# A two-layer decoder on one core: the first layer's values projected for all heads at once, ahead of the head pairs

## The reference, cut to what matters

```python
h = rmsnorm(x, mixer_norm[0])
parts = split_cols(h @ even_w_in[0], [ATTN_W] * N_DIL + [ATTN_W, ATTN_W, CROSS_WIDTH])   # 3 q, k, v, cross q
mix = mixer_dilated(parts[:N_DIL], parts[N_DIL], parts[N_DIL + 1], rel_bias)
cross = cross_attention(parts[N_DIL + 2], mem_n, w_mem_kv[0])
x = x + jnp.concatenate([mix, cross], axis=-1) @ w_out[0]
```

## Time and profile before

| | |
|---|---|
| median of 3 runs | 1532.45 us (1531.69 to 1534.11) |
| profiled execution: its own time | 1534.58 us |
| its span, first to last instruction | 1532.8 us |
| PE busy | 1513.6 us, 99% |
| VectorE, ScalarE, POOL busy | 86%, 73%, 6% |
| TensorE clock, mean granted | 0.996 |
| first projection of pair 0 starts | 37.96 us |
| layer 0's attention ends on PE | 231.1 us |

### The profile page before, as it was taken

The page is one execution under the profiler, slowest core; times in us unless marked ns, Lnnn a source line. Parts: engine busy times, 40 slices in busy tenths (PEclk is TensorE's granted clock), DMA queues, the critical chain, the costliest instruction groups (busy, mean ns, idle before and its releaser), DMA issues.

```text
span 1532.8 us, 25011 instructions
## 1 busy us (share of the span) xinstructions
PE 1513.6 (99%) x8132; PEld 1280.9 (84%) x8132; DVE 1316.3 (86%) x1783; ACT 1124.7 (73%) x1487; POOL 95.3 (6%) x70
## 2 busy tenths in 40 slices
PE   9999999999999999999999999999999999999997
PEld 8999978888898788888888888888888888888886
DVE  5788868777778879998998998998998998998997
ACT  6565566544557668788788888788788888878875
POOL 2422100000030000000000000000000000000000
PEclk9999999999999989999999999999999999999999
DMA  9944546666633579999999999999999999999992
GB/s 283 241 138 137 152 129 190 190 186 192 170 90 90 164 291 369 391 380 390 381 369 389 378 374 385 380 377 376 382 396 360 384 395 358 387 391 352 401 385 112
DMA packets 225973, 455.39 MB, mean 297 GB/s; under 512 B 12848, under 2 KB 119488, under 8 KB 225920
## 3 DMA queue, kind: packets, MB, share of 16 engines
q1 hardware_dynamic: 221712, 439.52, 79.5%
q0 software_dynamic: 4208, 15.22, 3.9%
HBM read 445.52 MB, written 9.18 MB: 297 GB/s over the span
## 4 chain that ended last, share of the span: by engine, by line
PE 93%; DVE 4%; ACT 1%; issue 1%; DMA 0%; SPq 0%; ACTq 0%; DVEq 0%
PE ps L815 26%; PE ps L817 26%; PE ps L816 26%; PE ps L1139 5%; PE ps L1141 3%; PE ps L1327 2%; PE ps L931 2%; PE ps L967 1%; PE ps L947 1%; DVE w_lo L1824 1%; PE ps L1269 0%; DMA big<-in_w_mem_kv 0%; DVE X L2030 0%; DVE small L1920 0%; DVE pr L2190 0%
## 5 line engine op out<-in xcount | busy, mean ns | idle before, releaser
L1824 DVE TENSOR_TENSOR w_lo<-big,w_hi 128x1024 fp32r<-128x1024 f32 (+1 forms) x830 | 977.6, 1217 | 121.4 <-ACT w_hi L1711 52.2
L1711 ACT CAST w_hi<-big 128x1024 fp32r<-128x1024 f32 x672 | 693.5, 1056 | 139.1 <-PE ps L817 135.5
L815 PE MATMUL ps<-w_hi,m_hi 128*128 128x512 f32 (+1 forms) x1008 | 392.6, 389 | 1.5 <-DVE w_lo L1824 1.3
L817 PE MATMUL ps<-w_hi,m_lo 128*128 128x512 f32 (+1 forms) x1008 | 389.7, 387 | 0.0
L816 PE MATMUL ps<-w_lo,m_hi 128*128 128x512 f32 (+1 forms) x1008 | 389.6, 386 | 0.0
L815 PEld LDWEIGHTS ps<-w_hi,m_hi 128*128 128x128 f32 x1008 | 189.5, 188 | 41.5 <-issue 4.3
L817 PEld LDWEIGHTS ps<-w_hi,m_lo 128*128 128x128 f32 x1008 | 189.5, 188 | 38.2
L816 PEld LDWEIGHTS ps<-w_lo,m_hi 128*128 128x128 f32 x1008 | 189.6, 188 | 36.9
L1364 ACT CAST w_hi<-big 128x1024 fp32r<-128x1024 f32 (+2 forms) x166 | 164.8, 1003 | 39.5 <-PE ps L817 32.4
L815 PE MATMUL ps<-w_hi,h_two 128*128 128x512 f32 (+1 forms) x464 | 182.1, 392 | 0.0
L817 PE MATMUL ps<-w_hi,h_two 128*128 128x512 f32 (+1 forms) x464 | 179.5, 387 | 0.0
(11 more groups left out here) (309 smaller groups left out, 1560.6 us busy)
## 6 DMA issues: line engine op xcount, KB each, us to landing
big<-in_odd_w_gate SPq DMA_DIRECT2D x112, 1024.0 KB, 7.3
big<-in_odd_w_up SPq DMA_DIRECT2D x112, 1024.0 KB, 7.7
big<-in_odd_w_down SPq DMA_DIRECT2D x112, 1024.0 KB, 7.6
big<-in_even_w_in SPq DMA_DIRECT2D x42, 512.0 KB, 4.3
big<-in_even_w_gate SPq DMA_DIRECT2D x22, 512.0 KB, 4.6
big<-in_even_w_up SPq DMA_DIRECT2D x22, 512.0 KB, 3.9
big<-in_even_w_down SPq DMA_DIRECT2D x22, 512.0 KB, 4.7
big<-in_w_out SPq DMA_DIRECT2D x20, 512.0 KB, 3.7
```

Source lines behind the costliest of these rows:

```text
L815: mm(dst, a[0], b[0], start=start, stop=False, **kw)
L817: return mm(dst, a[1], b[0], start=False, stop=stop, **kw)
L1711: nc.scalar.copy(w_hi[:, slot, :], ring[s][:, (u % 2) * UNIT:(u % 2 + 1) * UNIT]).then_inc(s_hi, 1)
L1824: return V.tensor_tensor(dst, src, lead.bitcast(F32), ALU.subtract)
```

## The change

- The values of all 16 heads are made before pair 0: eight units `("values", c)`, one per chunk of 128 input features, with full rows of 1024 value columns. The tokens' chunk is the loaded operand and the weights are streamed, so the values come out with tokens on partitions and are copied (four copies of 512 columns) into `XH`, from which `mix` reads them. `turn_values`, `vN` and two copies per pair go.
- A pair has four matrices instead of five. The step on PE is `p(0, 1, 2)`, `turn_probs(now, 0)`, `p(3)`, `turn_probs(now, 1)`, `scores(nxt)`, `mix(now)`. `third_read` is waited for at `p(1)` instead of `p(0)`.
- The second head's division moves from DVE to ACT (`second_probs`).
- For pair 1 the fourth low part comes after the first reading of scores; inside the steps there is no fifth low part after the reading.
- In pair 7's step PE makes output units 0 and 1 instead of unit 0; pair 8's step makes 2 and 3 instead of 1, 2 and 3.
- On ACT the second head's exponentials stand ahead of the second projection's copy.
- PE's steps are written out instead of looped.

```diff
+        for c in range(DC):
+            add(("values", c), (c + 2) % SLOTS)
         for g in range(PAIRS):
-            for m in range(NBR + 2):
+            for m in range(NBR + 1):
                 add(("pair", 0, g, m), m)
...
+            def values_unit(c):
+
+                w = split(0, 0, [U.at[("values", c)]], 1)
+                pe.wait_ge(s_nlo, DC * NORM_MIX0 + c + 1)
                 for t in range(TT):
-                    last = tr(value_bank(pair)[:, tok(t)], vT[:, tok(t)], ident)
-                last.then_inc(S["turned_v"], 1)
+                    if c == 0:
+                        pe.wait_ge(s_me, 2 * t + 2)
+                    for hf in range(2):
+                        last = mm3(value_bank(t, hf), part(HS, A_, c, tok(t)), part(w, A_, 0, slice(hf * 512, (hf + 1) * 512)),
+                                   c == 0, c == DC - 1, skip_group_check=True)
+                        if c == DC - 1 and (t, hf) != (1, 1):
+                            last.then_inc(s_vmade, 1)
+                last.then_inc(s_used, 1)
...
-                if isinstance(now.g, int) and now.g >= LATE:
-                    ahead = {LATE: ((), (0,)), LATE + 1: ((1, 2), (3,)), LATE + 2: ((4, 5), (6,))}[now.g]
+                if now.g >= LATE:
+                    ahead = {LATE: ((0,), (1,)), LATE + 1: ((2,), (3,)), LATE + 2: ((4, 5), (6,))}[now.g]
                     if not now.cross:
                         project(nxt, 0)
-                        turn_values(now)
                         project(aft, 0)
...
-                p(0)
-                turn_values(now)
-                p(1)
+                p(0, 1, 2)
                 turn_probs(now, 0)
-                p(2, 3)
+                p(3)
                 turn_probs(now, 1)
                 scores(nxt)
-                p(4)
                 mix(now)
...
+            def second_probs(pair):
+
+                S = s_at[0]
+                act.wait_ge(S["summed"], 2 * pair.g + 2)
+                act.wait_ge(S["dve_rden"], 2 * pair.g + 2)
+                for t, (a, b) in enumerate(((0, P), (P, CAUSAL))):
+                    last = A(probs(pair, 1)[:, a:b], tmp[:, a:b], ACT.Copy, scale=rden[:, 1, t:t + 1])
+                last.then_inc(S["probs"], 1)
...
                     e(0)
-                    values()
                     h(0)
+                    exps(now, 1)
                     e(1)
-                    exps(now, 1)
                     h(1)
+                    e(2)
                     probsT(now, 0)
-                    e(2)
+                    second_probs(now)
                     h(2)
                     e(3)
+                    h(3)
                     probsT(now, 1)
-                    h(3)
-                    e(4)
                     h(4)
```

More of the change, by code:

```diff
@@ L620, in stream_loads @@
                 span = range(1, PAIRS // 2)
+                for c in range(DC):
+                    load(0, 0, [U.at[("values", c)]], w_in[0][:, c:c + 1, (NBR + 1) * D:(NBR + 2) * D])
                 load_pair(pair_at(0, 0))
@@ L759, in _ @@
             mask_pair(0, 0, True)
-            u = U.at[("pair", 0, 1, NBR + 1)]
+            u = U.at[("pair", 0, 1, NBR)]
             mask_pair(1, 1, True)
@@ L957, in mix @@
                 elif pair.l == 0:
-                    pe.wait_ge(S["values"], pair.g + 1)
-                    v = vN[:, :, :]
+                    v = XH[:, :, pair.g * P:(pair.g + 1) * P]
                 else:
@@ L1035, in stream @@
                 first = pair_at(0, 0)
+                for c in range(DC):
+                    values_unit(c)
                 for m in range(first.mats):
-                    project(first, m, norm if m == 0 else None)
-                pe.wait_ge(s_me, 2 * 2)
+                    if m < 2:
+                        pe.wait_ge(s_vout, m + 1)
+                    project(first, m)
+                pe.wait_ge(s_vout, 2 * TT)
                 scores(first)
-                steps(pe, step)
+                for g in range(NPAIR):
+                    step(pair_at(0, g), *(pair_at(0, h) if h < NPAIR else None for h in (g + 1, g + 2)))
                 for ch in range(LATE, NPAIR):
@@ L1473, in e @@
                         evac((nxt, aft)[m], 0)
-                def values():
-                    if not now.cross:
-                        act.wait_ge(S["turned_v"], now.g + 1)
-                        nc.scalar.copy(vN[:, :, :].rearrange("p t n -> p (t n)"), value_bank(now)).then_inc(S["values"], 1)
                 exps(now, 0)
@@ L1544, in step_odd, with values_out, stream @@
                     mix_hi(g)
-            def stream(done):
+            def values_out(t, hf):
+                if (t, hf) != (1, 1):
+                    act.wait_ge(s_vmade, 2 * t + hf + 1)
+                else:
+                    act.wait_ge(s_used, U.at[("values", DC - 1)] + 1)
+                nc.scalar.copy(XH[:, t, hf * 512:(hf + 1) * 512], value_bank(t, hf)).then_inc(s_vout, 1)
+            def stream():
                 act.sem_inc(s_at[0]["probsT"], 1)
                 a, b = pair_at(0, 0), pair_at(0, 1)
-                for m in range(done, a.mats):
+                for c in range(2, DC):
+                    hi(0, 0, [U.at[("values", c)]])
+                for m in range(3):
                     hi_mat(a, m)
+                for t in range(TT):
+                    for hf in range(2):
+                        values_out(t, hf)
+                hi_mat(a, 3)
                 for m in range(a.mats):
@@ L1580, in _ @@
                 hi(0, 0, [U.at[("mem", n)]])
-            for m in range(3):
-                hi_mat(pair_at(0, 0), m)
+            for c in range(2):
+                hi(0, 0, [U.at[("values", c)]])
             mem_out(1)
             act.wait_ge(s_scrw, 16)
-            stream(3)
+            stream()
             def half_copy(i, first, ns):
@@ L1941, in head_probs @@
                     dve.wait_ge(S["probs_turned"], n + 1)
+                if pair.kind == "even" and hh:
+                    return
                 for t, (a, b) in enumerate(((0, n0), (n0, n0 + SEQ))):
@@ L1955, in step @@
                     low(0)
-                    if isinstance(now.g, int) and now.g == LATE:
-                        head_probs(now, 1)
-                        low(1)
-                    else:
-                        low(1)
-                        head_probs(now, 1)
+                    head_probs(now, 1)
+                    low(1)
                     low(2)
```

45 lines of the change are left out of this document (21 added, 24 removed).

## The result

The changed kernel takes 1537.88 us (median of 8 runs, 1536.59 to 1538.85); the kernel before takes 1534.06 us beside it (8 runs, 1531.37 to 1534.25). The ratio is 1.0029, 95% interval 1.0019 to 1.0038: slower by 0.29%, some 4.4 us (the medians differ by 3.8). I had forecast no change, and the median lies 0.3 us above the range. Of the 5.0 us between my 1532.9 and 1537.88, 1.6 come from the kernel before, whose median I had from three runs (1532.45); the other 3.4 are the change. The profiled execution took 1536.94 us, 2.36 more than that of before.

A forecast was written before the change was run, and what follows sets the result against it. PE, busy 99% of the span, was taken as the bound. Terms 22.1 - 2.4 - 0.7 - 19.4 + 0.8 summed to +0.4 us, giving 1532.9 us for the median, range 1530.3 to 1537.6.

The forecast's parts named there:

- Term 1: Values for all heads ahead of pair 0: 96 matmuls of 0.2306 us on PE add 22.1 us.
- Term 2: Pair 0: one matrix less, partly offset by an uncovered wait for the key's copy, saves 2.4 us.
- term 3: From pair 0's scores to pair 1's: less PE work, limited by DVE's fourth low part, saves 0.7 us.
- Term 4: Six steps from pair 1's scores to pair 7's: each 3.2 us shorter, at 15.61 us, saving 19.4 us.
- the walk from E: One step timed from a score block's end, E: ACT and DVE keep up, with no slack at the key's copy.
- Term 5: From pair 7's scores on: matmuls saved, but PE stands 3.7 us before output unit 0; adds 0.8 us.
- The rival of ScalarE: In the steps, ACT's division and cast delay the key's copy, 0.6 us a step: 1537.1 us, chance 0.13.
- The rival of the clock: After the 3.7 us stall in pair 7's step, PE's clock halves for 8.2 us: +4.1, 1537.0 us, chance 0.10.

The follow-up runs named there:

- bias_at_scores: Changed kernel, but POOL's three bias additions of a step wait for the next pair's scores instead of the second head's probabilities: 1534.50 us.
- copy_first_all: Changed kernel, but in every even step ScalarE copies the second projection ahead of the second head's exponentials: 1531.57 us.
- div_on_dve: Changed kernel, but with the second head's division back on VectorE: 1538.69 us.
- low3_behind: Changed kernel, but the fourth low part stands behind the reading of the next pair's scores in every step: 1540.94 us.
- before_collide: Kernel before the change, but POOL's bias additions wait for the second head's exponentials instead of its probabilities: 1549.82 us.
- copy_first_last: Changed kernel, but in pair 7's step alone ScalarE copies pair 9's query ahead of the second head's exponentials: 1533.96 us.
- key_covered: Changed kernel with POOL's additions at the scores, second projection's copy first, four matrices before both probability transposes, key copied before turned probabilities: 1533.85 us.

## Why the prediction was right and wrong

- **Term 1** (+22.1, measured +21.75): right. The 96 matmuls take 21.86 us (37.85 to 59.71), 0.228 each, close to the row's 0.2306; no load held them up. The rule with which the prediction gets 0.216 is given in the Trainium skill, "TensorE: Matmul & The Clock Gate", section "Back-to-back issue gap", for an isolated matmul and not for a stream of them; the trace gives 0.228.
- **Term 2** (-2.4, measured -2.31) and **term 3** (-0.7, measured -0.94): right. Pair 0's scores start at 71.89 where I had 72.1.
- **Term 4** (-19.4, measured -16.05): wrong, and with it the sign of the result. The step that failed is the walk from E, "DVE starts to read at E+0.35 and ends the second head's maxima at E+6.1", and its end, "So all fits". It priced every low part at its length alone, 1.25 us, and left POOL out. It also left out that the fourth matrix needs bank 4 back from the second query, whose copy the change had put behind the second head's exponentials; by the walk's own times (copy done some 0.35 after E+9.3, matrix at E+9.8) that would have cost nothing, and it is where the delay shows. In the trace the reading starts at E+1.08 and the exponentials end at E+9.9 (164.76), not E+9.3. Without the collision the step is 15.54, where I had 15.61: the blocks were right. The division, taken as 0.7, took 0.81 (166.59 to 167.40). Rows for the collision stood in the trace of before, the two quoted above: POOL's additions wait for exactly the probabilities that the change moves to another engine, and a low part beside them takes 1.61 us.
- **Term 5** (+0.8, measured +2.05): the gap was right (3.54 for 3.7), and the term lacked the slower matmuls behind it, 1.6 us.
- **The rival of ScalarE** (steps of 16.0 or more would "prove" it): the steps did come to 16.17, with another cause. `bias_at_scores` shows that ScalarE's work alone did not set them; `copy_first_all` shows that it is a part of the loop that did (0.28 us a step for one copy). I had tied a mechanism to a number that a second mechanism gives as well; only its releaser, the key's copy, would have told it apart, and the trace has another.
- **The rival of the clock** (+4.1, 0.10): it happened, at 1.6 us. That gap was forecast in the sum itself, so what follows it belonged there too, with more than a chance of 0.10. Its price was too high, because it took over the length of another stretch (8.2 us).
- **The range:** the terms named for it add up to 1530.5 and 1537.0, where the prediction writes 1530.3 and 1537.6.
- **The sum:** +0.4 forecast, +3.35 for the steps, +1.25 for the end and -0.5 for the smaller misses give the +4.5 of the table. Removing both causes gives 1529.80, 8.1 us under the changed kernel and 0.33% under the kernel before. The change holds a gain of some 4 us and gives away twice that in two orders that it did not need.

## What to carry to other kernels

When a change moves an operation to another engine, list every wait on its semaphore, also on engines that are idle 94% of the time, and ask what will run beside the work that it starts. A wait's place on the bound engine shows where the delay arrives, not where it is made: look for the loop among the other engines, and cut it there. And a gap of 2 us or more on PE is to be priced with the slower matmuls that may stand behind it: 1.6 us here, behind two of the five gaps of 2.16 us and behind each of the four of 3.5 us or more (there 1.6 to 2.4).

## What the runs showed of the hardware

- A VectorE operation with two SBUF inputs and a POOL addition of SBUF operands exclude each other, instruction by instruction: low parts of 1.22 us take up to 2.30, additions of 0.54 take 1.57, and POOL's of 1.28 take 2.27. VectorE's operations with a PSUM input (0.41, 0.55 and 0.68 us) and its maxima of one input (0.55 and 0.94) kept their lengths beside POOL in `bias_at_scores`.
- Who starts first decides who pays: in the step of the kernel before it was POOL (2.09 us for the first addition), in the changed kernel both.
- After 3.54 us without a matmul (the changed kernel and `bias_at_scores`), and after 3.56 and 4.68 (`div_on_dve`, `low3_behind`), PE ran at 1.2 GHz when it started again. After the five gaps of 2.16 us in the steps of `before_collide` it started at its upper level; behind two of them it fell to 1.2 GHz 1.2 to 1.4 us later, behind three it did not. After gaps of 0.46 (`copy_first_last`), 1.55 and 1.65 us (`before_collide`, `key_covered`) it did not fall. The Trainium skill, "TensorE: Matmul & The Clock Gate", section "HAM oscillation — how this bites in real kernels", says that idle gaps between bursts of matmuls put the clock to its lower level; these runs agree for the gaps of 3.54 us and more (clock 0.50 to 0.62 behind them), and for those of 2.16 us in two cases of five; what decides between these is not shown.
